# One piece of every expert's weights is loaded as nine row combs instead of one block

## The chip, the cores and the metric

The kernel runs on one core of a Trainium2 chip. The metric is the device time of one execution, in microseconds (us). Three runs of the kernel before gave 1218.85, 1219.08 and 1220.23 us, a median of 1219.08 us. "GB/s" is what the core's 16 DMA engines moved together.

## The reference, cut to what matters

A two-layer decoder trunk over 256 tokens of width 1024, all in float32. The first layer has latent attention and a dense SwiGLU, the second one sliding-window attention and a mixture of eight SwiGLU experts, of which each token uses two. The part that the change touches is the last one:

```python
D_MODEL, SEQ, N_EXPERTS, TOP_K, D_FF_EXPERT = 1024, 256, 8, 2, 3584

def moe(xn, w_router, w_gate, w_up, w_down):
    logits = (xn @ w_router).astype(jnp.float32)
    top_val, top_idx = lax.top_k(logits, TOP_K)
    top_w = jax.nn.softmax(top_val, axis=-1)
    gates = jnp.sum(jax.nn.one_hot(top_idx, N_EXPERTS, dtype=jnp.float32) * top_w[..., None], axis=-2)

    def per_seq(args):
        xs, gs = args
        hg = jnp.einsum('sd,edf->sef', xs, w_gate)
        hu = jnp.einsum('sd,edf->sef', xs, w_up)
        hh = jax.nn.silu(hg) * hu * gs[..., None].astype(xs.dtype)
        return jnp.einsum('sef,efd->sd', hh, w_down)

    return lax.map(per_seq, (xn, gates))
```

All eight experts get tokens, so all their weights are read: 8 experts x 3 matrices x 1024 x 3584 float32 numbers, 352 MB.

## The kernel before, in words

The first 400 us are attention, the dense layer and the router. The rest is the expert phase. There an item is one expert with up to 96 gathered tokens. Its weights come as 24 pieces (`pieces`, line 558) of 128 partitions x 3584 numbers, 1792 KB each: pieces 0 to 7 are the gate matrix, 8 to 15 the up matrix, 16 to 23 the down matrix (four for each half of the hidden width). A piece is one row of 14336 contiguous bytes for each partition. The pieces go round a ring in SBUF that holds eight of them (`LAPS`), so a piece can be loaded once the piece eight before it has been read by TensorE.

SyncE (SP) issues all of these loads, in order, in `load_item` (line 700). `room_for` makes it wait until TensorE has read the piece that lay there. The load itself is line 718; only the last piece, number 23, is split into two halves by columns (lines 721 and 722), the second of which counts on a semaphore of its own, `tail_landed`. Every load adds 16 to the semaphore of its ring place (`landing(m, first)`) when it has landed. Each of the DMA engines that carry a load adds one to it behind its own rows; I call such an addition a mark.

TensorE (PE) works item by item (`pe_item`, line 1638): products with gate (line 1575), with up (the same line), then the down product in 28 rows of 1024 columns, `down` at line 1603, 14 rows, the gather for the next item (line 1541), and 14 more rows. In a narrow item (at most 64 tokens) a down row is two matmuls, lines 1618 and 1619; in a wide one it goes through `wide_step` (lines 1550 to 1554). A down row waits for the pieces that it needs: row 14 is the first of piece 20, row 21 the first of piece 22, row 24 the first that reads piece 23, and rows 26 and 27 read its second half. VectorE and ScalarE make the hidden activations between the up and the down product (lines 2113 and 2118).

ScalarE issues loads of its own at the start (lines 823 to 835), on another queue of the same DMA engines: eight tables of 16, 16, 8, 3, 2, 1, 8 and 8 rows, one row for each partition, and the 256 positions, one number at a time. At the end it issues a quarter of the output, 128 rows.

The program has eight items in this execution; the first one (`load_item(0, 0, True)`) has four of its pieces in other places, loaded ahead, and the other seven are a loop.

Of the kernel before, what the change touches and what calls it, by code (L numbers as in the profile page):

```python
# [37 lines left out]
P = 128  # L38
# [91 lines left out]
class Semaphores:  # L130
    def __init__(self, sem):
# [125 lines left out]
        self.ahead_loaded_b = sem("ahead_loaded_b")  # L257
        self.ahead_loaded_c = sem("ahead_loaded_c")
        self.tail_landed = sem("tail_landed")
        self.gu_read = sem("gu_read")  # L260
        self.gate_mm = sem("gate_mm")
        self.sg_ready = sem("sg_ready")
# [21 lines left out]
def build(nc, x, positions, w_in, g_q, g_kv, w_uq, w_ukv, w_o, kv_g, kv_w, kv_b, swa_w_q, swa_b_q,  # L284
          swa_sinks, swa_w_o, swa_b_o, rel_bias, g_attn, g_ffn, f_gate, f_up, f_down, w_router,
          e_gate, e_up, e_down, g_final, consts, out):
    with ExitStack() as ctx:
# [12 lines left out]
        s = Semaphores(lambda name: ctx.enter_context(nc.semaphore(name)))  # L300
# [257 lines left out]
        pieces = [(kind, 0, k) for kind in "gu" for k in range(KD)]  # L558
        pieces += [("d", half, part) for half in range(2) for part in range(TILES * D // PIECE)]
        NP = len(pieces)  # L560
        DOWN0 = 2 * KD
        assert NP % LAPS == 0 and KD == LAPS
        ppos = {p_: m for m, p_ in enumerate(pieces)}
        whole = ring[:].rearrange("p a n -> p (a n)")

        def turn_of(m, first):

            return sum(1 for p_ in range(m) if p_ not in AHEAD) if first else m - OUTSIDE

        def place(m, first):  # L570

            return PIECE * ((FIRST_AT + turn_of(m, first)) % LAPS)

        def landing(m, first):

            return s.piece_landed[turn_of(m, first) % LAPS]
# [5 lines left out]
        def piece_here(eng, i, m, first):  # L582

            if first and m in AHEAD_A:
                eng.wait_ge(s.ahead_loaded_a, 16 * len(AHEAD_A))
            elif first and m in AHEAD_B:
                eng.wait_ge(s.ahead_loaded_b, 16)
            elif first and m in AHEAD_C:
                eng.wait_ge(s.ahead_loaded_c, 16)
            else:  # L590
                eng.wait_ge(landing(m, first), i * (16 * NP // LAPS) + 16 * (turn_of(m, first) // LAPS + 1))

        def piece(m, first):
            if first and m in AHEAD:
                return AHEAD[m]
            return whole[:, place(m, first):place(m, first) + PIECE]

        def down_row(r):

            c0 = (place(DOWN0, False) + D * r) % (LAPS * PIECE)  # L600
            return whole[:, c0:c0 + D]

        def down_pieces(r):

            return range(DOWN0 + D * r // PIECE, DOWN0 + (D * r + D - 1) // PIECE + 1)

        def last_down_row(m):

            return (PIECE * (m + 1 - DOWN0) - 1) // D

        def in_tail(r):

            return D * r + D > PIECE * (NP - DOWN0) - PIECE // 2

# [45 lines left out]
        def _(sp):  # L660
# [11 lines left out]
            def piece_of_expert(m, expert):  # L672
                kind, half, part = pieces[m]
                if kind == "d":
                    return ed[:, expert, half, part * PIECE:(part + 1) * PIECE]
                return (eg if kind == "g" else eu)[:, expert, part, :]

            def room_for(i, m, first):

                if first and turn_of(m, True) < LAPS:  # L680
                    for sl in dense_under(m):
                        if sl >= 5:
                            sp.wait_ge(*used_up(NU - 1))
                        else:
                            sp.wait_ge(*stream[earlier_fill(DENSE, sl)][4:6])
                    return
                if not first and m < LAPS:
                    sp.wait_ge(s.down_mm, i * (2 * TILES) + (last_down_row(m + 2 * LAPS) + 2 - 2 * TILES))
                    return
                under = m - LAPS  # L690
                if first:
                    in_ring = [p_ for p_ in range(NP) if p_ not in AHEAD]
                    under = in_ring[in_ring.index(m) - LAPS]
                kind, _, k = pieces[under]
                if k < KD - 1:
                    sp.wait_ge(s.gu_read, i * (2 * KD - 2) + ((KD - 1) * (kind == "u") + k + 1))
                else:
                    sp.wait_ge(s.gate_mm if kind == "g" else s.up_mm, i * (2 * THIRDS) + 2 * THIRDS)

            def load_item(i, expert, first):  # L700
                for m in range(NP):
                    if first and m == 5:
                        sp.wait_ge(s.spT_mm, AH)
                        for ma, room in AHEAD_A.items():
                            sp.dma_start(room, piece_of_expert(ma, expert)).then_inc(s.ahead_loaded_a, 16)
                        sp.wait_ge(s.spv_mm, MH)
                        for ma, room in AHEAD_B.items():
                            sp.dma_start(room, piece_of_expert(ma, expert)).then_inc(s.ahead_loaded_b, 16)
                    if first and m == LAPS + 1:
                        sp.wait_ge(s.swo_mm, 4)  # L710
                        sp.wait_ge(s.router_mm, 2)
                        for ma, room in AHEAD_C.items():
                            sp.dma_start(room, piece_of_expert(ma, expert)).then_inc(s.ahead_loaded_c, 16)
                    if first and m in AHEAD:
                        continue
                    room_for(i, m, first)
                    if m < NP - 1:
                        sp.dma_start(piece(m, first), piece_of_expert(m, expert)).then_inc(landing(m, first), 16)
                    else:
                        src, mid = piece_of_expert(m, expert), PIECE // 2  # L720
                        sp.dma_start(piece(m, first)[:, 0:mid], src[:, 0:mid]).then_inc(landing(m, first), 16)
                        sp.dma_start(piece(m, first)[:, mid:PIECE], src[:, mid:PIECE]).then_inc(s.tail_landed, 16)

            load_item(0, 0, True)
            sp.wait_ge(s.counts_ready, 1)
            sp.wait_ge(s.order_ready, 1)
            with sp.Fori(1, NE) as i:
                load_item(i, sp.value_load(order[0:1, bass.ds(i, 1)], min_val=0, max_val=NE - 1), False)
# [8 lines left out]
            rows = out[0].rearrange("(t p) d -> t p d", p=P)  # L737
# [348 lines left out]
        def _(pe):  # L1086
# [39 lines left out]
            for half in range(2):  # L1126
# [22 lines left out]
                for t in range(TT):  # L1149
                    for k in range(3):  # L1150
                        r = w[:, k, :].rearrange("p (h n) -> p h n", n=192)[:, :, NOPE:192]
# [21 lines left out]
            for n in range(4):  # L1173
                t, half = n // 2, n % 2
                for k in range(2):
                    r = w[:, k, :].rearrange("p (h n) -> p h n", n=256)[:, 4 * half:4 * half + 4, NOPE:256]
# [370 lines left out]
            def wide_step(bank, slots, left, right, first, last):  # L1547
                thirds = [slots[:, 32 * j:32 * j + 32] for j in range(3)]
                for j in range(3):
                    pe.matmul(ps[32 * j:32 * j + 32, bank, :], thirds[j], left, start=first, stop=last)  # L1550
                pe.matmul(ps[SLOTS:P, bank, :], thirds[2], right, start=first, stop=last)  # L1551
                for j, cols in ((0, 0), (1, 0), (0, LASTQ), (1, LASTQ)):
                    q = 32 * j + cols // 4
                    mm = pe.matmul(ps[q:q + 32, bank + 1, 0:LASTQ], thirds[j], right[:, cols:cols + LASTQ], start=first, stop=last)  # L1554
                return mm
# [47 lines left out]
            def down(i, half, j, narrow, first_item):  # L1603
                r = half * TILES + j
                for m in down_pieces(r):
                    if r == 0 or m not in down_pieces(r - 1):
                        piece_here(pe, i, m, first_item)
                if in_tail(r) and not in_tail(r - 1):
                    pe.wait_ge(s.tail_landed, i * 16 + 16)
                if r == 0:  # L1610
                    pe.wait_ge(s.sgt_ready, i + 2)
                if j == 0:
                    pe.wait_ge(s.hhT_ready, i * 2 + (half + 1))
                w = down_row(r)
                first, last = r == 0, r == 2 * TILES - 1
                if narrow:
                    lhs = hhT[:, half, j, 0:NARROW]
                    pe.matmul(ps[0:NARROW, DOWN_BANK, :], lhs, w[:, 0:512], start=first, stop=last)  # L1618
                    mm = pe.matmul(ps[64:64 + NARROW, DOWN_BANK + 1, :], lhs, w[:, 512:1024], start=first, stop=last)  # L1619
                else:  # L1620
                    mm = wide_step(DOWN_BANK, hhT[:, half, j, :], w[:, 0:512], w[:, 512:1024], first, last)
                mm.then_inc(s.down_mm, 1)
# [555 lines left out]
```

## Time and profile before

| What | us |
|---|---|
| median of three runs | 1219.08 |
| the profiled execution | 1220.05 |
| its span, first to last instruction | 1218.2 |
| TensorE busy in the span | 1167.6 |
| share of the DMA engines' time, SP's loads | 82.1% |
| expert phase, rate of the DMA engines | about 425 GB/s |

The span is 1.85 us shorter than the execution's own time. The row of tenths for DMA in the page has a 9 for each slice from the fifteenth to the last but one, and TensorE has 8 or 9 in the same slices, so the shares of busy time alone don't say which of the two sets the time. That is read from waits and from the times at which loads landed. An issue's time to landing runs from SP's issue to the last mark of the load, so with many loads queued it is mostly time in the queue.

### The profile page before, as it was taken

To read this page: it belongs to the slowest core of one execution; us is meant where nothing else is said; L and a number is where in the kernel's file an instruction comes from. 1 tells how busy PE (TensorE), PEld (TensorE's weight loads), DVE (VectorE), ACT (ScalarE), POOL (GpSimd) and SP (SyncE) were. 2 spreads that over 40 slices of the span, in tenths; PEclk is the share of its full clock that TensorE was granted. 3 is DMA by queue.
4 is the path that set the end of the run, shared out by engine and by line. 5 is a ranking of instruction groups with operands and counts; after the bars stand their busy time and mean duration, and the time that the engine had idled before them with its cause. 6 is when DMAs were issued, how large, how long until landed. Compare 5 with 4: busy or idle time off the path is not lost.

```text
span 1218.2 us, 21794 instructions
## 1 busy us (share of the span) xinstructions
PE 1167.6 (96%) x9461; PEld 586.6 (48%) x9462; DVE 338.9 (28%) x727; ACT 213.2 (17%) x399; POOL 36.0 (3%) x67
## 2 busy tenths in 40 slices
PE   7999999999999999899899999899999889999987
PEld 4878777778765534233233433333343233334323
DVE  3666566666272302101002011010201101020112
ACT  2454333333263100000010010101010010101001
POOL 2130000000200000000000000000000000000000
PEclk9999999999999999899899999999999999999999
DMA  9624645237535899999999999999999999999994
GB/s 339 244 69 162 230 161 188 89 139 257 219 122 241 358 425 406 420 428 425 425 425 426 417 421 426 426 426 426 424 426 425 426 427 426 424 425 408 427 426 171
DMA packets 56044, 413.42 MB, mean 339 GB/s; under 512 B 4703, under 2 KB 10077, under 8 KB 32141
## 3 DMA queue, kind: packets, MB, share of 16 engines
q1 hardware_dynamic: 54464, 410.40, 82.1%
q8 instruction: 81, 1.33, 0.4%
q0 software_dynamic: 944, 1.29, 0.3%
q10 hardware_dynamic: 540, 0.29, 0.1%
q14 instruction: 15, 0.11, 0.0%
HBM read 410.91 MB, written 1.05 MB: 338 GB/s over the span
## 4 chain that ended last, share of the span: by engine, by line
PE 82%; DMA 9%; DVE 4%; issue 2%; ACT 2%; ACTq 0%; POOL 0%; POOLq 0%; DVEq 0%; SPq 0%
PE ps L1575 35%; PE ps L1550 6%; PE ps L1618 6%; DMA ring<-in_moe_w_gate 5%; DMA ring<-in_moe_w_down 4%; PE ps L1262 4%; PE ps L1258 4%; PE ps L1259 4%; PE ps L1554 3%; PE ps L1593 3%; PE ps L1434 2%; PE ps L1541 2%; PE ps L1385 2%; PE ps L1121 2%; ACT w_hi L918 1%
## 5 line engine op out<-in xcount | busy, mean ns | idle before, releaser
L1575 PE MATMUL ps<-ring,arena 128*32 128x448 f32 x4736 | 460.9, 548 | 11.4 <-issue 7.1
L1575 PEld LDWEIGHTS ps<-ring,arena 128*32 128x32 f32 x4736 | 154.3, 111 | 310.5 <-issue 307.3
L1618 PE MATMUL ps<-ring,arena 128*64 128x512 f32 x280 | 125.3, 601 | 15.0 <-DMA ring<-in_moe_w_down 11.0
L1619 PE MATMUL ps<-ring,arena 128*64 128x512 f32 x280 | 125.3, 602 | 0.0
L2113 DVE TENSOR_TENSOR arena<-arena,ps 128x448 f32<-128x448 f32 x38 | 22.3, 603 | 285.1 <-PE ps L1575 284.7
L1550 PE MATMUL ps<-ring,arena 128*32 128x512 f32 x504 | 87.0, 593 | 2.4 <-DVE arena L2118 2.4
L1859 DVE TENSOR_TENSOR w_lo<-ring,w_hi 128x2048 fp32r<-128x2048 f32 x31 | 71.0, 2292 | 57.1 <-ACT w_hi L918 55.1
L1551 PE MATMUL ps<-ring,arena 128*32 128x512 f32 x168 | 85.9, 593 | 0.0
L1618 PEld LDWEIGHTS ps<-ring,arena 128*64 128x64 f32 x280 | 37.4, 138 | 96.1 <-issue 71.4
L918 ACT CAST w_hi<-ring 128x2048 fp32r<-128x2048 f32 x31 | 59.1, 1909 | 112.6 <-PE ps L1262 112.6
L2095 DVE TENSOR_TENSOR h<-h,ps 128x512 f32<-128x512 f32 x36 | 24.7, 687 | 175.5 <-PE ps L1593 175.5
L1258 PE MATMUL ps<-w_hi,xT_hi 128*128 128x512 f32 (+1 forms) x176 | 64.9, 376 | 0.0
L1259 PE MATMUL ps<-w_hi,xT_lo 128*128 128x512 f32 (+1 forms) x176 | 63.9, 370 | 0.0
L1030 ACT ACTIVATE arena<-ps 128x448 f32<-128x448 f32 x38 | 20.7, 544 | 246.1 <-PE ps L1575 245.4
L1037 ACT ACTIVATE arena<-ps,vecT 128x96 f32<-128x96 f32 x36 | 9.3, 342 | 309.0 <-PE ps L1541 309.0
L1554 PE MATMUL ps<-ring,arena 128*32 128x256 f32 x672 | 51.7, 379 | 0.0
L1554 PEld LDWEIGHTS ps<-ring,arena 128*32 128x32 f32 x672 | 21.8, 110 | 50.3 <-issue 50.3
L1262 PE MATMUL ps<-w_lo,xT_hi 128*128 128x512 f32 (+1 forms) x176 | 41.4, 379 | 0.0
L2129 DVE TENSOR_TENSOR arena<-ps,vecT 128x384 f32<-128x384 f32 x8 | 4.5, 557 | 119.5 <-PE ps L1541 119.5
L1619 PEld LDWEIGHTS ps<-ring,arena 128*64 128x64 f32 x280 | 37.4, 138 | 0.0
L1541 PEld LDWEIGHTS ps<-arena,xn 128*128 128x128 f32 x288 | 34.5, 200 | 5.6 <-issue 5.3
L1258 PE MATMUL ps<-w_hi,fhhT_hi 128*128 128x512 f32 x88 | 34.7, 395 | 1.4 <-DVE h L1928 1.4
(309 smaller groups left out, 1193.9 us busy)
## 6 DMA issues: line engine op xcount, KB each, us to landing
ring<-in_moe_w_gate SPq DMA_DIRECT2D x63, 1792.0 KB, 18.9
ring<-in_moe_w_up SPq DMA_DIRECT2D x61, 1792.0 KB, 18.4
ring<-in_moe_w_down SPq DMA_DIRECT2D x56, 1792.0 KB, 20.9
ring<-in_moe_w_down SPq DMA_DIRECT2D x16, 896.0 KB, 21.2
ring<-in_ffn_w_gate SPq DMA_DIRECT2D x5, 2048.0 KB, 7.9
ring<-in_ffn_w_up SPq DMA_DIRECT2D x5, 2048.0 KB, 7.7
ring<-in_ffn_w_down SPq DMA_DIRECT2D x5, 2048.0 KB, 7.9
ring<-in_mla_w_o SPq DMA_DIRECT2D x2, 2048.0 KB, 24.8
```

The source lines that it names most:

```text
L918: act.copy(hi, w).then_inc(s.whi_ready, 1)
L1258: pe.matmul(out, lhs[0][:, k, c], rhs_hi[:, k, :], start=(first and k == 0), stop=False)
L1259: pe.matmul(out, lhs[1][:, k, c], rhs_hi[:, k, :], start=False, stop=False)
L1262: mm = pe.matmul(out, lhs[0][:, k, c], rhs_lo[:, k, :], start=False, stop=(last and k == nk - 1))
L1541: mm = pe.matmul(ps[:, GATHER_BANK + k // 4, (k % 4) * SLOTS:(k % 4 + 1) * SLOTS], xn[:, t, k * P:(k + 1) * P], sel[:, t, :], start=(t == ...
L1550: pe.matmul(ps[32 * j:32 * j + 32, bank, :], thirds[j], left, start=first, stop=last)
L1551: pe.matmul(ps[SLOTS:P, bank, :], thirds[2], right, start=first, stop=last)
L1554: mm = pe.matmul(ps[q:q + 32, bank + 1, 0:LASTQ], thirds[j], right[:, cols:cols + LASTQ], start=first, stop=last)
L1575: mm = pe.matmul(ps[Q * q:Q * q + Q, bank_of(a, j), 0:CH], lhs, w[:, c0:c0 + CH], start=first, stop=last)
L1618: pe.matmul(ps[0:NARROW, DOWN_BANK, :], lhs, w[:, 0:512], start=first, stop=last)
L1619: mm = pe.matmul(ps[64:64 + NARROW, DOWN_BANK + 1, :], lhs, w[:, 512:1024], start=first, stop=last)
L1859: dve.tensor_tensor(lo, w, hi.bitcast(F32), ALU.subtract).then_inc(s.wlo_ready, 1)
```

## The change

Piece 22, the last but one, is no longer one load of 128 rows. Seven loads take the partitions 0, 8, ..., 120, then 1, 9, ..., 121, and so on to 6, 14, ..., 126: 16 rows each, 8 partitions apart. Two more take the 16 rows that are left, in two sets of 8 rows 16 partitions apart: 7, 23, ..., 119 and 15, 31, ..., 127. The first of the nine counts on the piece's own semaphore, the other eight on a new one, `comb_landed`. TensorE waits for both before the first down row that reads the piece. The same bytes go from the same place to the same place, and nothing is computed otherwise.

```diff
         NP = len(pieces)
+        COMBED, TEETH = NP - 2, 8
+        FULL_COMBS = [slice(r, P, TEETH) for r in range(TEETH - 1)]
+        HALF_COMBS = [slice(r, P, 2 * TEETH) for r in (TEETH - 1, 2 * TEETH - 1)]
+        COMBS = FULL_COMBS + HALF_COMBS
         DOWN0 = 2 * KD
...
                     room_for(i, m, first)
-                    if m < NP - 1:
+                    if m == COMBED:
+                        room, src = piece(m, first), piece_of_expert(m, expert)
+                        for rows in COMBS:
+                            sp.dma_start(room[rows, :], src[rows, :]).then_inc(landing(m, first) if rows == COMBS[0] else s.comb_landed, 16)
+                    elif m < NP - 1:
                         sp.dma_start(piece(m, first), piece_of_expert(m, expert)).then_inc(landing(m, first), 16)
...
                     if r == 0 or m not in down_pieces(r - 1):
                         piece_here(pe, i, m, first_item)
+                        if m == COMBED:
+                            rest = 16 * (len(COMBS) - 1)
+                            pe.wait_ge(s.comb_landed, i * rest + rest)
```

On SP, in the body of the loop over the experts, pieces 21, 22 and 23 stood as follows before (lines 718, 721 and 722 are the loads, ISA rows set up registers or wait):

```order
L718 DMA ring<-in_moe_w_down 128x3584
L696 REGISTER_ALU
L718 ISA
L718 DMA ring<-in_moe_w_down 128x3584
L721 ISA
L721 DMA ring<-in_moe_w_down 128x1792
L722 ISA
L722 DMA ring<-in_moe_w_down 128x1792
```

In the changed kernel the same place reads so (line 725 is the comb's load, 730 and 731 the halves of piece 23):

```order
L727 DMA ring<-in_moe_w_down 128x3584
L701 REGISTER_ALU
L725 ISA
L725 DMA ring<-in_moe_w_down 16x3584
...
L725 DMA ring<-in_moe_w_down 8x3584
L725 ISA
L725 DMA ring<-in_moe_w_down 8x3584
L730 ISA
L730 DMA ring<-in_moe_w_down 128x1792
L731 ISA
L731 DMA ring<-in_moe_w_down 128x1792
```

Eight more loads and their register instructions now stand ahead of piece 23.

On PE, in the narrow branch of the loop, the first down row that reads piece 22 stood so before, with what it waits for (`piece_landed2` is the semaphore of the piece's ring place):

```order
L1619 MATMUL ps<-ring,arena 64x512
L1618 MATMUL ps<-ring,arena 64x512 [waits piece_landed2]
L1619 MATMUL ps<-ring,arena 64x512
L1618 MATMUL ps<-ring,arena 64x512
```

And now:

```order
L1631 MATMUL ps<-ring,arena 64x512
L1619 ISA [waits piece_landed2]
L1630 MATMUL ps<-ring,arena 64x512 [waits comb_landed]
L1631 MATMUL ps<-ring,arena 64x512
L1630 MATMUL ps<-ring,arena 64x512
```

One instruction that only waits has come ahead of the matmul; nothing else moved on PE, and nothing on the other engines.

## Rows read from the trace of the kernel before

**Rows 1.** The page: the DMA engines in 40 slices.
```profile
DMA  9624645237535899999999999999999999999994
GB/s 339 244 69 162 230 161 188 89 139 257 219 122 241 358 425 406 420 428 425 425 425 426 417 421 426 426 426 426 424 426 425 426 427 426 424 425 408 427 426 171
```
**Rows 2.** Busy time by stretch: length, each engine, PE's clock, DMA share, GB/s.
```profile
core 0: us, PE busy (x) PEld busy (x) DVE busy (x) ACT busy (x) POOL busy (x), PEclk, DMA share, GB/s
789.02:893.63 104.61, 103.59 (x1070) 39.45 (x1074) 12.66 (x21) 5.17 (x13) 0.00 (x0) 0.98 1.01 425
893.63:998.24 104.61, 96.93 (x858) 35.18 (x850) 11.45 (x20) 7.78 (x15) 0.00 (x0) 1.00 1.01 426
485.00:1182.00 697.00, 669.53 (x6350) 244.70 (x6346) 82.39 (x140) 43.49 (x89) 0.00 (x0) 0.99 1.01 424
```
**Rows 3.** SP's loads on line 718: issue to landing, whole span, then 485 to 1172 us.
```profile
DMA to landing us min/median/max: 7.1/19.3/32.1
DMA to landing us min/median/max: 9.2/20.5/32.1
```
**Rows 4.** The chain of waits: start us, us, what (a load: issue to landing).
```profile
761.43 27.59 DMA ring<-in_moe_w_gate
943.42 23.14 DMA ring<-in_moe_w_down
967.98 30.26 DMA ring<-in_moe_w_gate
1155.49 26.73 DMA ring<-in_moe_w_down
```
**Rows 5.** DMA queues from 789.02 to 998.24 us: packets, MB, share of 16 engines.
```profile
q1 hardware_dynamic: 7249, 88.76, 100.2%
q8 instruction: 16, 0.26, 0.5%
```
**Rows 6.** The single loads issued at 940.27 and 1152.49: KB, us to landing.
```profile
ring<-in_moe_w_down SPq DMA_DIRECT2D x1, 1792.0 KB, 22.0
ring<-in_moe_w_down SPq DMA_DIRECT2D x1, 1792.0 KB, 23.6
```
**Rows 7.** Last item's piece 23: SP's timeline, then each half's KB and us to landing.
```profile
1171.01 0.33 SPq L721 DMA_DIRECT2D ring<-in_moe_w_down  x1
1171.53 0.33 SPq L722 DMA_DIRECT2D ring<-in_moe_w_down  x1
ring<-in_moe_w_down SPq DMA_DIRECT2D x1, 896.0 KB, 30.2
ring<-in_moe_w_down SPq DMA_DIRECT2D x1, 896.0 KB, 31.9
```
**Rows 8.** The page: ScalarE's queue: packets, MB, share of 16 engines.
```profile
q10 hardware_dynamic: 540, 0.29, 0.1%
```
**Rows 9.** TensorE's timeline at the last item's down rows.
```profile
1182.27 0.76 PE L1618 MATMUL ps<-ring,arena 128*64 128x512 f32 x1 [2.45 <-DMA ring<-in_moe_w_down]
...
1182.82 1.06 PE L1618 MATMUL ps<-ring,arena 128*64 128x512 f32 x1
...
1183.67 1.06 PE L1618 MATMUL ps<-ring,arena 128*64 128x512 f32 x1
...
1204.21 0.59 PE L1618 MATMUL ps<-ring,arena 128*64 128x512 f32 x1
...
1204.64 0.59 PE L1618 MATMUL ps<-ring,arena 128*64 128x512 f32 x1
```
**Rows 10.** Busy time by stretch, as Rows 2, in the last item.
```profile
1182.00:1186.00 4.00, 3.73 (x10) 1.16 (x12) 0.00 (x0) 0.00 (x0) 0.00 (x0) 0.58 1.03 437
1186.00:1190.00 4.00, 4.00 (x20) 1.15 (x16) 0.00 (x0) 0.00 (x0) 0.00 (x0) 0.99 0.98 416
```
**Rows 11.** TensorE's waits for loads: total us, times, longest us.
```profile
PE ps L1618 <- DMA ring<-in_moe_w_down: 11.0, 7, 2.4
PE ps L1575 <- DMA ring<-in_moe_w_gate: 4.4, 2, 2.2
```

More of the change, by code:

```diff
@@ L259, in __init__ @@
         self.tail_landed = sem("tail_landed")
+        self.comb_landed = sem("comb_landed")
         self.gu_read = sem("gu_read")
```

## The prediction, written before the changed kernel ran

> **What bounds the kernel now.** First the page, its slices by time: from the fifteenth slice to the last but one the DMA engines are busy nine tenths or more and move 402 to 430 GB/s [rows 1]. Then busy time by stretch: from 485 to 1182 us the DMA share is 1.01 at 424 GB/s, while TensorE is busy 669.5 of 697 us, so it has 27.5 us to spare and the DMA engines have none [rows 2]. Then the times to landing: in that stretch no load landed sooner than 9.2 us after its issue, and the fastest of all, which had no queue ahead of it, took 7.1 [rows 3]. So work was always queued. The end of the last load is set by how fast the queue drains, and TensorE's waits for loads are only 15.4 us in all [rows 11], because the ring lets it run behind or catch up. What ends last is the stream of weights.
>
> Then how evenly it drains. The chain of waits gives the landings of two experts' first gate pieces: 761.43 + 27.59 = 789.02 and 967.98 + 30.26 = 998.24, two experts apart [rows 4]. That is 104.61 us for one expert. Two neighbouring plain pieces landed at 940.27 + 22.0 = 962.3 and 943.42 + 23.14 = 966.56, 4.3 us apart [rows 4, 6], so 24 of them need 103.2 us. The slowest engine loses the other 1.4 us of each expert. It shows as single steps: 1152.49 + 23.6 = 1176.1 and 1155.49 + 26.73 = 1182.22 are 6.1 us apart, 1.8 more than plain [rows 4, 6]. Beside the weights there are 16 instruction packets in two experts, 0.26 MB [rows 5], so eight for an expert of 16 KB each. Spread evenly they would cost each of 16 engines 8 KB, which at 426/16 = 26.6 GB/s is 0.3 us. A loss of 1.4 us on the slowest says that some engines carry them all. A piece has landed when its slowest engine is done, so the others run ahead by about 1.1 us (1.4 less 0.3) for each expert or more, and their lead is worth nothing.
>
> **The change part by part.**
> *Rows on engines.* A plain piece is 128 rows on 16 engines, eight each, 4.3/8 = 0.54 us a row. How many engines a small load uses can be counted. ScalarE's queue has 540 packets [rows 8]: 62 table rows, 256 positions and 128 output rows are 446, and 94 are left, which is 16+16+8+3+2+1+8+8 for the tables and 16+16 for the other two. So a load of 16 rows leaves 16 marks, one of 8 rows leaves 8. A full comb gives each engine one row. The two half combs give one half of the engines two rows and the other half none: nine rows against seven, where all had eight. The Trainium skill has this rule too ("DMA: Bandwidth & Descriptors", "Why a DMA increments its semaphore by 16 and not by 1"), and adds that SyncE's loads take the lowest-numbered engines; by that, the seven-row half would always be the same one. The packets agree with the count; which engines they are no row shows.
> If the half that gets seven rows is the one that carries the instructions, the slowest engines gain 0.54 us for each expert; if it is the other, they lose it.
> *More loads.* Seven marks instead of one on an engine with seven rows, nine on the others. Piece 23 is already two loads: its halves landed at 1171.01 + 30.2 = 1201.2 and 1171.53 + 31.9 = 1203.4, 2.2 apart against 4.3/2 = 2.15 [rows 7]. So an extra load costs an engine between 0 and 0.1 us, and I take 0.02, since the halves differ from half a piece by less than the reading's last digit. Six extra: 0.12, leaving 0.54 - 0.12 = 0.42 us gained for each expert (between 0 and 0.54).
> *Rate of a combed row.* The trace has no large load of fewer than 128 partitions, so it bounds nothing here but by its plain rows: 0.54 us at best, and if engines stand in each other's way two by two, 1.07. I take 0.54, the row's measured price, for the forecast; the other end is a rival below.
> *Issue.* SP's two halves are issued 1171.53 - 1171.01 = 0.52 apart [rows 7]; eight more loads are 4.2 us of SP. Behind them stand piece 23 and, for the next expert, piece 0. Piece 23 was issued about 3 us after piece 22, held by TensorE's reading, so it comes 9 x 0.52 - 3.0 = 1.7 us later. What hides it is the queue: loads took a median of 20.5 us to land where 7.1 would do [rows 3]; at the tightest, 9.2, 2.1 us of cover are left. Without it, up to 1.7 us per expert.
> *The wait on PE.* `comb_landed` holds down rows 21 to 27 and all products behind them. It comes due when the last comb row lands, as the old wait did, and the waiting instruction is one of some 1650: nothing beyond the landing itself.
>
> *The end.* In the last item TensorE starts its down row at 1182.27 after waiting 2.45 us for piece 18 [rows 9], and from there computes without a wait for loads to 1206. Seven combs lie ahead of that piece: 7 x 0.42 = 2.9 us. After that wait TensorE's granted clock reads 0.58 for 4 us, next to 0.99 behind it [rows 10]: between 1.2 and 2.4 GHz, mostly the lower, with the engine idle before it. A step there takes 1183.67 - 1182.82 = 0.85 us instead of 1204.64 - 1204.21 = 0.43 [rows 9], 1.7 us in those 4 us. A wait shortened by the earlier arrival (it was one of several; the engine then gets there earlier too) may not cost the clock: 0 to 1.4 us, as then the last half of piece 23, landing 8 x 0.42 = 3.4 us earlier at 1200.0, becomes what row 26 waits for (it starts at 1204.21 now [rows 9]). I take 0.8.
> Sum: 2.9 + 0.8 = 3.7 us less. Against the profiled execution's 1220.05 that is 1216.4. The median of the runs is 0.97 below that execution, so I forecast 1215.5 us in its terms, own range 1213 to 1218.
>
> **Rivals.**
> *The combs collide (slower).* In a plain piece each engine's rows lie in partitions that no other engine writes. A comb hands its rows to engines in another pattern, and the 16 rows may lie in fewer places of SBUF than there are engines. Its place is piece 22; it decides as soon as two engines that share a place are slowed by more than the 0.42 us gained. If all comb rows take double, an engine with nine rows needs 18 row times instead of 8: 5.4 us more, 103.2 + 5.4 = 108.6 against 104.6, 4.0 for each expert, 32 over eight: 1251. Half of that where some pairs are out of step (1235), and more where engines knocked out of order then meet in the plain pieces (1262). For it: nothing in the trace contradicts it, and the rate of 26.6 GB/s for an engine may as well be that of the place it writes. Against it: no row shows it. The Trainium skill says exactly this ("SBUF — State Buffer", "Door 1: The DMA port swizzle"): 16 ports, each of 8 partitions in two groups of four 32 apart, at 27.2 GB/s each. By its table partitions 8 apart reach 8 of the 16 ports, which makes the doubling above; no run here shows it.
> *The wrong half.* The nine-row half is the one with the instructions: 0.54 + 8 x 0.02 = 0.70 more for each expert, seven of them ahead of piece 18: 4.9 us, 1224. For it: the rows leave the half open. Against it: only the skill's numbering, which doesn't say where instructions travel either.
> *Nothing to see.* An extra load costs nearer 0.09 than 0.02, six of them eat the 0.54, or SP's 4.2 us empty the queue where it is short: 1219. For it: the reading allows up to 0.1 for a load. Against it: the halves' 2.2.
>
> **How the numbers follow.** Forecast 0.45, collision 0.32, wrong half 0.09, nothing 0.14. What a measurement can tell from no change is about 0.2%, 2.4 us. Of the forecast's 0.45, 0.04 lie within it (a gain of under 2.4): faster 0.41, same 0.14 + 0.04 = 0.18, slower 0.41. The range must reach from the forecast's lower end to deep in the collision: 1213 to 1262 leaves out the worst of the knock-on and a gain of over 6. The cases have both signs: the likeliest's own range is 1213 to 1218.
>
> **What would show it.** Right: first gate pieces of neighbouring experts land 104.2 us apart instead of 104.61, GB/s by stretch rises from 425 to 426 or 427, TensorE's wait before 1182 is under 2.45. Collision: in each expert one stretch of some 10 us with the GB/s well under 400 where piece 22 is moved, and experts 107 to 110 us apart. Wrong half: 105.3 us apart with no dip. The issue term is wrong if the DMA share falls under 1 behind piece 22. The whole is wrong if TensorE, and not a landing, ends the wait ahead of most down rows.

## The result, and the profile after

| | before | after |
|---|---|---|
| median of the runs | 1218.96 us (4 runs, 1218.83 to 1220.23) | 1311.43 us (4 runs, 1300.29 to 1312.42) |
| ratio | | 1.0731, interval 1.0709 to 1.0753: slower |
| span of the profiled execution | 1218.2 us | 1310.6 us |

The forecast was 1215.5 us with a range of 1213 to 1262. The kernel lost 92 us and lies outside the range, on the side of the rival "the combs collide", but 49 us past its worst figure. Three of the four runs lie between 1310.9 and 1312.4 us and one at 1300.3; nothing here explains that one, and a single run of a changed kernel can therefore be off by some 12 us.

The page's DMA slices (as [rows 1], a slice is now 32.8 us), then TensorE's longest waits for loads (us in total, times, longest; lines 1584 and 1630 are 1575 and 1618 of the kernel before):

```profile
DMA  9516444348159999999999999999999999999991
GB/s 342 203 62 249 160 169 161 129 161 313 58 231 374 415 330 425 428 319 426 426 379 346 425 428 274 419 425 371 317 426 426 290 388 401 406 284 426 425 313 67
```
```profile
PE ps L1630 <- DMA ring<-in_moe_w_down: 53.4, 22, 5.9
PE ps L1584 <- DMA ring<-in_moe_w_up: 25.4, 25, 1.2
PE ps L1584 <- DMA ring<-in_moe_w_gate: 10.6, 10, 2.4
```

The busy row of the DMA engines has not changed: nines to the end. The GB/s row has: where before it stood at 425, there is a dip every three or four slices, eight in all, one for each expert. Whoever reads only the busy share sees nothing. TensorE waits 89.4 us for loads where it waited 15.4 [rows 11]. The chain of waits gives the landings of first gate pieces of every other expert, as in [rows 4]:

```profile
558.20 37.88 DMA ring<-in_moe_w_gate
...
787.72 43.52 DMA ring<-in_moe_w_gate
...
1025.66 43.00 DMA ring<-in_moe_w_gate
```

They land at 596.08, 831.24 and 1068.66 us: 117.6 and 118.7 us an expert where it was 104.61. Inside a dip (SyncE's comb loads of this expert start at 674.97), busy time by stretch:

```profile
core 0: us, PE busy (x) PEld busy (x) DVE busy (x) ACT busy (x) POOL busy (x), PEclk, DMA share, GB/s
660.00:676.00 16.00, 16.00 (x176) 5.52 (x172) 0.41 (x1) 0.00 (x0) 0.00 (x0) 1.00 1.00 425
...
684.00:688.00 4.00, 4.00 (x56) 1.65 (x52) 0.09 (x1) 0.00 (x0) 0.00 (x0) 1.00 0.97 201
...
696.00:700.00 4.00, 4.00 (x47) 2.52 (x40) 0.00 (x0) 0.00 (x0) 0.00 (x0) 1.00 1.00 253
...
704.00:708.00 4.00, 4.00 (x52) 1.56 (x48) 0.00 (x0) 0.00 (x0) 0.00 (x0) 1.00 0.99 419
```

201 GB/s is half of 425, the engines are busy all the while (0.97), and the stretch lasts some 22 us (680 to 702, 242 GB/s on average). Piece 22 has 1.8 MB, which at half rate is 8.7 us. So two things are to be explained: the half rate, and why it lasts more than twice as long as the piece.

### The profile page after: what moved, and what is told of

Its sections match the earlier page's. It is cut to its first block, busy times and chain, and to the rows that moved or that the text cites. A ratio compares the mean times of both kernels' runs of the same rounds, so it can differ in the third digit from the quotient of the medians.

```text
span 1310.6 us, 21978 instructions
## 1 busy us (share of the span) xinstructions
PE 1186.2 (91%) x9461; PEld 584.6 (45%) x9462; DVE 339.0 (26%) x727; ACT 213.1 (16%) x399; POOL 36.0 (3%) x67
## 4 chain that ended last, share of the span: by engine, by line
PE 63%; DMA 29%; DVE 3%; issue 2%; ACT 2%; ACTq 0%; POOL 0%; POOLq 0%; DVEq 0%; SPq 0%
PE ps L1584 25%; DMA ring<-in_moe_w_gate 12%; DMA ring<-in_moe_w_down 10%; DMA ring<-in_moe_w_up 7%; PE ps L1559 4%; PE ps L1271 4%; PE ps L1267 4%; PE ps L1268 4%; PE ps L1630 3%; PE ps L1443 2%; PE ps L1563 2%; PE ps L1602 2%; PE ps L1394 2%; PE ps L1130 2%; PE ps L1550 1%
## 5 line engine op out<-in xcount | busy, mean ns | idle before, releaser
L1584 PEld LDWEIGHTS ps<-ring,arena 128*32 128x32 f32 x4736 | 151.0, 111 | 349.3 <-issue 286.8
L1630 PE MATMUL ps<-ring,arena 128*64 128x512 f32 x280 | 141.0, 656 | 54.5 <-DMA ring<-in_moe_w_down 53.4
L1631 PE MATMUL ps<-ring,arena 128*64 128x512 f32 x280 | 141.0, 656 | 0.0
L1630 PEld LDWEIGHTS ps<-ring,arena 128*64 128x64 f32 x280 | 39.6, 150 | 149.3 <-issue 75.6
L1563 PEld LDWEIGHTS ps<-ring,arena 128*32 128x32 f32 x672 | 21.8, 110 | 50.3 <-issue 50.3
L1631 PEld LDWEIGHTS ps<-ring,arena 128*64 128x64 f32 x280 | 39.6, 150 | 0.0
```

Source lines behind the costliest of these rows:

```text
L1584: mm = pe.matmul(ps[Q * q:Q * q + Q, bank_of(a, j), 0:CH], lhs, w[:, c0:c0 + CH], start=first, stop=last)
```

## The experiments

The theories. A: the 16 rows of a comb lie in fewer places of SBUF (sets of partitions that are filled through one door) than there are engines, and each place takes in only what one engine brings. B: the same on the side of the weights in HBM. C: the number of loads (or SyncE's issues, or marks). D: the split of 9 rows to 7. Later K and U: engines that are out of step (some of them behind the others in the queue) make a comb dearer than by itself. In the run with one comb, K stands for another thing, that every comb costs the same.

**Patterns by themselves.** A kernel of loads only, four pieces for each pattern; the kernel's computation is left out. The pattern is a list of row slices:

```python
COMB8 = every(8, 16, range(8))              # eight loads of 16 partitions, 8 apart
BLOCK = every(1, 16, range(0, P, 16))       # eight loads of 16 adjacent partitions
LOW_COMB = every(16, 8, range(16))          # sixteen loads of 8 partitions, 16 apart
LOW_SPREAD = every(4, 8, [b + r for b in (0, 32, 64, 96) for r in range(4)])   # 8 partitions, 4 apart
# columns: seven loads of 128 partitions x 512 columns
```

> This kernel leaves out all of the reference's computation: SyncE alone issues loads of the down weights, four pieces (1792 KB each) for each of eleven patterns, one pattern after the other with a wait between them, and stores x as its output. Theory A (engines that write into the same one of 16 groups of partitions share that group's rate): plain pieces 4.3 us each; eight combs of 16 rows 8 apart 8.4 each (8 groups reached); the same combs read from blocks of 16 adjacent rows also 8.4; blocks of 16 adjacent partitions 16.9 (4 groups); combs 7 apart about 6.8, read from rows 8 apart the same; 8-row loads 4 apart 8.6, 8-row loads 16 apart 16.9; columns 4.6 to 4.9; 64 rows 8.4; 112 and 16 rows 6.8. Theory B (the rows read in memory collide, not those written): the pattern of the source decides, so combs read from blocks differ from combs read from combs, and combs 7 apart read from rows 8 apart are as slow as combs 8 apart. Theory C (each further load costs an engine time): the time goes by the number of loads alone: 8 loads a piece all alike, whatever the spacing, columns with 7 as slow as they, 64 rows with 2 nearly plain.

SyncE's timeline (start us, length of the issues; the next pattern starts when all has landed), and the page's slices of 10.9 us:

```profile
5.62 1.87 SPq L32 DMA_DIRECT2D ring<-in_moe_w_down  x4
25.15 20.18 SPq L33 DMA_DIRECT2D ring<-in_moe_w_down  x32
61.80 20.09 SPq L34 DMA_DIRECT2D ring<-in_moe_w_down  x32
98.09 14.98 SPq L35 DMA_DIRECT2D ring<-in_moe_w_down  x32
158.25 19.85 SPq L36 DMA_DIRECT2D ring<-in_moe_w_down  x32
192.09 19.82 SPq L37 DMA_DIRECT2D ring<-in_moe_w_down  x32
225.38 43.11 SPq L38 DMA_DIRECT2D ring<-in_moe_w_down  x64
271.92 38.77 SPq L39 DMA_DIRECT2D ring<-in_moe_w_down  x64
339.73 14.00 SPq L40 DMA_DIRECT2D ring<-in_moe_w_down  x28
362.26 4.97 SPq L41 DMA_DIRECT2D ring<-in_moe_w_down  x8
399.21 3.88 SPq L42 DMA_DIRECT2D ring<-in_moe_w_down  x8
431.73 0.41 SPq L66 DMA_DIRECT2D out<-res  x1
```
```profile
GB/s 245 429 230 213 221 168 210 213 187 128 127 126 126 128 145 241 228 178 247 231 149 162 170 165 146 114 109 113 114 109 113 242 391 192 216 217 171 261 231 196
```

From one start to the next, divided by four: plain 4.9 us a piece, combs 9.2 (33), combs fed from adjacent rows of the weights 9.1 (34), adjacent blocks 15.0 (35), combs 7 apart 8.5 (36; 8.3 from other source rows, 37), eight-row combs 4 apart 11.6 (38, held by SyncE, which issues 64 loads in 43.1 us), eight-row combs 16 apart 17.0 (39), strips of columns 5.6 (40), two loads of 64 rows 9.2 (41), 112 and 16 rows 8.1 (42). The rates are levels: 429, then about 213, then 127, then 109 to 114. B falls (33 and 34 agree) and so does C (28 strips are nearly as fast as plain). What counts is which partitions a load covers. If combs lie in eight places and eight-row combs 16 apart in four, a place takes in 27 GB/s (213/8, 110/4), which is what one engine carries (425/16). Here "The Trainium skill" ("SBUF — State Buffer", "Door 1: The DMA port swizzle") states 16 ports of 27.2 GB/s; combs and eight-row combs agree, adjacent blocks (127 GB/s, by that page four ports) lie 17% above it. Which partitions share a place no run here maps out.

The trace also has the time of each row's packet (14 KB), and it shows the collision without the issues of SyncE and without the wait at a pattern's end. The median is 0.54 us in plain pieces, 1.09 in combs (1.08 when fed from adjacent rows), 1.80 in adjacent blocks, 1.10 in two loads of 64 rows. Eight-row combs 4 apart take 0.54 and eight-row combs 16 apart 1.09, with the same number of loads, rows and marks. So an engine is not slow in small loads as such, and not in every partition that it does not write in a plain piece, or blocks would cost a row no more than combs do. A's sizes hold less well: combs 7 apart were expected at 6.8 us a piece and took 8.5, the 112 and 16 rows at 6.8 and took 8.1, blocks at 16.9 and took 15.0.

**The kernel with other patterns.** Against after, only the lists of row slices change, and in one run the source rows:

```diff
# e1_eight_full_combs
-        HALF_COMBS = [slice(r, P, 2 * TEETH) for r in (TEETH - 1, 2 * TEETH - 1)]
+        FULL_COMBS = [slice(r, P, TEETH) for r in range(TEETH)]; HALF_COMBS = []
# e2_seven_apart
+        FULL_COMBS = [slice(r, 7 * 16, 7) for r in range(7)]
+        HALF_COMBS = [slice(7 * 16 + r, P, 2) for r in range(2)]
# e3_combs_from_blocks: comb n is loaded from 16 (or 8) adjacent rows of the weights
-    sp.dma_start(room[rows, :], src[rows, :])
+    sp.dma_start(room[rows, :], src[block_rows, :])
# e4_three_loads: as e2, the seven combs as one load
+        FULL_COMBS = [slice(0, 7 * 16)]
# e6_blocks
+        FULL_COMBS = [slice(16 * r, 16 * r + 16) for r in range(8)]; HALF_COMBS = []
```

> Eight combs of 16 rows, 8 partitions apart, and no 8-row loads: each engine has eight rows of piece 22 again. Theory A (shared groups of partitions): still slow, 1290 to 1320 us, since the combs are what collides. Theory D (the nine-and-seven split put more work on the slow half, or loads of 8 rows are slow themselves): back to 1219 to 1225. Theory C (number of loads): about 1300, like the changed kernel with its nine.

1312.0 us, one run like all of this group (before on that chip 1221.3). Nothing gained by leaving out the half combs: D falls.

> The changed kernel with its seven 16-row combs 7 partitions apart (they cover partitions 0 to 111) and the two 8-row loads on partitions 112 to 127; number and size of the loads are the same. Theory A: it moves, because the rows of a comb now lie in 14 groups instead of 8, but engines no longer meet the same partner from row to row, so somewhere between 1265 and 1305 us. Theory C (number of loads or marks): unchanged, 1308 to 1315. Theory D (nine and seven): unchanged, 1308 to 1315.

1320.1 us, outside what A expected, and 5 us outside what C and D did. In the quiet kernel (loads only) combs 7 apart had missed A's figure too, but were no dearer than combs 8 apart (8.5 against 9.2). So the miss is one of size, and the kernel adds something to a pattern's own cost.

> The changed kernel with the same destination rows in each load, but read from as many adjacent rows of the weights (the down product is then computed with rows of piece 22 in another order). Theory A (write side): unchanged, 1300 to 1315 us. Theory B (read side: rows 448 KB apart in memory collide): back to 1215 to 1225.

1314.9 us: B falls in the kernel too. (The rows of piece 22 then lie in another order, so this kernel computes something else than the reference; its loads and their times are what is compared.)

> Piece 22 as one load of partitions 0 to 111 (seven adjacent rows for an engine) and two loads of 8: three loads instead of nine, and each engine writes the same rows in the same order as in the run with combs seven apart (1320 us). Theory A: about 1320 again. Theory C (number of loads): a third of the cost, about 1250 or less.

1315.6 us with three loads instead of nine, as A expected; C's figure was 1250.

> Piece 22 as eight loads of 16 adjacent partitions: an engine still writes one row of each, but the 16 rows of a load lie in 4 places instead of 8. By itself such a piece took 15.0 us against 4.9 plain and 9.2 combed. Theory A: at least 8 x 10.2 = 81 us over the kernel before, 1300 or more, up to 1330. A rule that only strides are slow (a load of adjacent partitions is fast): 1222, as the strips.

1304.1 us. Blocks by themselves are 2.4 times as dear as combs (10.2 us over plain against 4.3) and in the kernel no dearer (one run, within the 1300 to 1312 us of the combed kernel's own). The half of A that says "slow" holds, the half that gives sizes does not.

**As many loads, other cut.**

```diff
-    for rows in COMBS: sp.dma_start(room[rows, :], src[rows, :])
+    for n in range(8): sp.dma_start(room[:, 448 * n:448 * n + 448], src[:, 448 * n:448 * n + 448])
```

> Piece 22 of each expert as eight loads of 128 partitions x 448 columns: as many loads and marks as eight full combs, but rows on engines as in a plain piece. Theory A (pattern of partitions): within 0.5% of the kernel before, 1216 to 1226 us (eight loads more would be at most 7 x 0.1 x 8 = 5.6 us). Theory C (the number of loads in a piece, or what SyncE spends on issuing them, makes the cost): near the 1312 us of the combs.

1221.78 us against 1219.55, ratio 1.0019 (1.001 to 1.0029). Eight loads cost almost nothing when the partitions are as in a plain piece. C falls for good, and the price of a load is had: in the strips' chain of waits

```profile
775.30 14.45 DMA ring<-in_moe_w_gate
...
985.58 14.20 DMA ring<-in_moe_w_gate
...
1160.65 27.15 DMA ring<-in_moe_w_down
```

two experts take 999.78 - 789.75 = 210.03 us, 0.4 an expert more than 104.61, for seven extra loads: 0.06 each.

**One comb piece alone.** Strips in all experts, eight full combs in the fourth only, then in the seventh only.

```diff
-    with sp.Fori(1, NE) as i: load_item(i, ...)
+    with sp.Fori(1, 3) as i: load_item(i, ...)          # 6 in the second kernel
+    load_item(3, ..., combed=True)
+    with sp.Fori(4, NE) as i: load_item(i, ...)
```

> As the strips, but the fourth expert's piece 22 alone is eight full combs. Theory A with nothing behind it: 4.2 us over the strips. Theory K, each comb costs the same by itself: (1312 - 1219) / 8 = 11.6 us over the strips. Theory G (the cost grows from comb to comb, as engines drift further apart): under 11.6 here, and the landings after it return to 4.3 us a piece.

1232.54 us, ratio to before 1.0106 (1.0089 to 1.0123), 10.8 over the strips. By landings, in its chain:

```profile
762.10 35.89 DMA ring<-in_moe_w_gate
...
993.88 14.20 DMA ring<-in_moe_w_gate
```

797.99 is 8.2 behind the strips' 789.75, and two experts later 1008.08 is 8.3 behind 999.78. One comb costs 8.2 us and stops costing. That is twice the piece by itself, and less than the 11.5 of after. The profiled run was the fastest of the four, 8.6 over the strips' profiled run; by the median alone K's 11.6 would not be excluded, and what excludes it is the landings of the next run and e1's chain.

> As the run with one comb piece in the fourth expert, but it is in the seventh. By itself there it cost 8 to 9 us by the landings behind it, with the engines 5 us apart before it; in the run with eight combed experts the costs grew from 7 (first) to 16 us (seventh), while the distance between first and last engine grew from 3 to 20 us. Theory U (what counts is how far engines are apart, which combs themselves enlarge): about 8 to 10 here, as engines are 7 us apart, 1230 to 1233. Theory L (late experts are dearer for another reason): 16, 1238.

1232.05 us (1.0106, 1.009 to 1.0123); piece 19 of its last expert lands at

```profile
1165.24 31.50 DMA ring<-in_moe_w_down
```

1196.74, 8.9 behind the strips' 1187.80. (The whole span is 10.7 behind. The other 1.8 come at the end: TensorE's granted clock reads 0.83 and 0.74 from 1195 to 1203 us, after a wait, and in the strips' run 1.00.) Late experts are not dearer by themselves. Combs behind combs are, as e1's chain shows:

```profile
556.69 37.24 DMA ring<-in_moe_w_gate
...
784.10 40.52 DMA ring<-in_moe_w_gate
...
1018.15 43.84 DMA ring<-in_moe_w_gate
```

824.62 and 1061.99 are 35.6 and 63.8 us behind [rows 4]: the first four combs cost 8.9 each, the next two 14.1 each. Meanwhile the sixteen engines' landing events for a first gate piece spread over 5, 7, 10, 14, 20 us from expert to expert, where the strips' spread over 3 to 8. From expert to expert these pieces land 113.0, 114.4, 116.3, 117.7, 119.7 and 121.0 us apart (strips 105.1). The change's own nine loads rise faster and level off: 113.7, 115.9, 119.3, 118.5, 118.9, 116.8.

**Out of step, in quiet.** Loads only again, 24 pieces a phase, each phase waited for as a whole.

```python
run([P_] * 24)                              # L72
run([P_] * 11 + [C_] + [P_] * 12)           # L73, C_: eight full combs
run([P_] * 11 + [C_] * 2 + [P_] * 11)       # L74
run([P_] * 11 + [H_] + [P_] * 12)           # L75, H_: the change's nine loads
run([SKEW] + [P_] * 24)                     # L76, SKEW: eight loads of 8 rows; then L77 to L79
```

> SyncE alone, nothing else runs; eight phases of 24 pieces, eleven pieces in flight, each phase waited for as a whole: (1) 24 plain; (2) a piece of eight full combs in the middle; (3) two such pieces in a row; (4) the change's own nine loads in the middle; (5) eight loads of 8 rows first, then 24 plain; (6) the same with a full-comb piece in the middle; (7) the same with the change's nine loads; (8) sixteen loads of 8 rows first and a full-comb piece. Theory A (places in SBUF are shared by engines while a comb is written, nothing else): 24 plain about 24 x 4.3 + 3 = 106 us; a comb +4.2, two +8.4, the nine loads +6.3; phase 5 +4.3 over phase 1 and phases 6, 7 +8.5 and +10.6. Theory K (knock-on: after a comb, or once engines are out of step, plain pieces behind it are slow too): a comb costs well over 4.2, up to the 11.5 us that an expert lost in the kernel, and two in a row cost less than twice one; engines out of step before it (6 to 8) make it dearer than (2).

```profile
5.75 60.01 SPq L72 DMA_DIRECT2D ring<-in_moe_w_down  x24
111.31 68.13 SPq L73 DMA_DIRECT2D ring<-in_moe_w_down  x31
221.36 74.53 SPq L74 DMA_DIRECT2D ring<-in_moe_w_down  x38
336.86 71.44 SPq L75 DMA_DIRECT2D ring<-in_moe_w_down  x32
448.33 72.31 SPq L76 DMA_DIRECT2D ring<-in_moe_w_down  x32
561.81 77.85 SPq L77 DMA_DIRECT2D ring<-in_moe_w_down  x39
680.10 78.14 SPq L78 DMA_DIRECT2D ring<-in_moe_w_down  x40
```

Starts give 105.6 us plain, 110.0 with a comb piece (+4.5), 115.5 with two (+9.9), 111.5 with the nine loads (+5.9). Engines in step pay just the comb: in the phase with two, the slices of 2.89 us show it, six of them at half rate, 17 us for two pieces of 8.7, and nothing behind.

```profile
GB/s 213 412 407 435 422 422 452 412 452 412 427 442 412 437 422 427 447 204 214 219 219 214 209 372 422 432 427 422 437 417 432 432 417 432 427 427 432 427 427 144
```

Phase L77 stood 4.8 above L76, and L78 (the nine loads) 6.1: no knock-on, it seemed.

The next run made four engines, or one, late in the same way:

> SyncE alone again, 24 pieces a phase; ahead of each phase some engines are made late by small loads: (1) eight loads of 4 rows, so that four engines are eight rows (4.3 us) late, then 24 plain; (2) the same, seventh piece in full combs; (3) the same, seventh and eighth in full combs; (4) four loads of 4 rows, then 24 plain; (5) the same with one comb piece; (6) eight loads of 1 row, so one engine is late, 24 plain; (7) with one comb piece; (8) as (1) with the change's own nine loads. Theory U (a comb's price depends on which engines are out of step with which, with no rule but that two engines on one place share its rate of one engine; worked out with that rule alone): comb +8.2 in (2), two combs +8.3 in (3), +6.2 in (5), +4.1 in (7), +8.8 in (8). Theory A alone (a comb costs what it costs in step): +4.5, +9.9, +4.5, +4.5, +5.9, as measured with the engines in step.

Differences of 3.8 (one comb), 7.9 (two), 3.3, 6.3 and 6.3: on neither theory. The fault is in the experiment. The small loads stood at a phase's start, where the queue is empty, and SyncE issues one in 0.6 us while an engine carries a row in 0.54. How late the engines were can be read from the time between the first and the last landing mark of a plain piece: 2.3 us in b2's L76, and in this run 1.3 with the comb but 2.8 without it (phases L75 and L74), so the two phases differ in more than the comb. Only the last pair but one (one engine, 3.3 us late in both phases) compares like with like, and there a comb cost 6.3. The other pairs tell little of engines out of step. Put behind three plain pieces, the small loads queue up:

```diff
-    run([E4] + [P_] * 24)
+    run([P_] * 3 + [E4] + [P_] * 21)                       # likewise SKEW, E1
+    run([P_] * 3 + [E4] + [P_] * 6 + [C_] + [P_] * 14)
```

> SyncE alone, 24 pieces a phase; now the small loads stand behind three plain pieces, so that the queue is never empty and the engines that carry them do get late: (1) eight loads of 8 rows (eight engines 4.3 us late) and plain pieces; (2) with one full-comb piece; (3) eight loads of 4 rows (four engines 4.3 us late), plain; (4) with one comb piece; (5) with two; (6) with the change's nine loads; (7) eight loads of 1 row, plain; (8) with one comb piece. Theory U (price of a comb depends on which engines are out of step; worked out with the one rule that two engines on one place share the rate of one): (2) - (1) = 4.1, (4) - (3) = 8.2, (5) - (3) = 8.3, (6) - (3) = 9.2, (8) - (7) = 4.1. Theory A alone, as in step: 4.5, 4.5, 9.9, 5.9, 4.5.

```profile
5.84 64.11 SPq L74 DMA_DIRECT2D ring<-in_moe_w_down  x32
115.57 76.66 SPq L75 DMA_DIRECT2D ring<-in_moe_w_down  x39
234.63 70.08 SPq L76 DMA_DIRECT2D ring<-in_moe_w_down  x32
346.66 78.79 SPq L77 DMA_DIRECT2D ring<-in_moe_w_down  x39
466.62 83.90 SPq L78 DMA_DIRECT2D ring<-in_moe_w_down  x46
590.79 82.07 SPq L79 DMA_DIRECT2D ring<-in_moe_w_down  x40
713.88 70.54 SPq L80 DMA_DIRECT2D ring<-in_moe_w_down  x32
825.22 77.56 SPq L81 DMA_DIRECT2D ring<-in_moe_w_down  x39
942.88 0.40 SPq L82 DMA_DIRECT2D out<-res  x1
```

By the marks of the plain pieces ahead of the comb, the engines are now 4.6 us apart with eight made late, 4.4 with four and 6.3 with one (meant were 4.3 each time), where L73 of b2 had 0.5. With eight engines late a comb piece costs 119.06 - 109.73 = 9.3 us, with four late 7.9 (two pieces 12.1, the change's nine loads 11.1), with one late 6.3; in step it was 4.5. That engines out of step raise the price is shown, with nothing else running, though each phase ran once. Behind the comb piece the marks stand 5.4, 4.4 and 8.0 us apart, and 6.2 behind the nine loads: most of these pieces leave the engines further apart than they found them. Theory U's one rule gives one of the sizes (8.2 for 7.9) and misses the others (4.1 for 9.3, 8.3 for 12.1, 9.2 for 11.1, 4.1 for 6.3), low each time.

**In step, in the kernel.** SyncE waits for piece 21 before it issues piece 22.

```diff
     if m == COMBED:
+        piece_here(sp, i, m - 1, first)
```

> The strips (1221.8 us), but SyncE waits for piece 21 to land before it issues piece 22, so that all engines are idle and then start piece 22 together. An unqueued load took 7.1 us against 4.3 of moving, so 2.8 us idle each time: 1221.8 + 8 x 2.8 = 1244 us. This is the base for the next run.

> Eight full combs (1312 us without the wait), with the same wait before them. Theory U: the engines start the combs in step, so a comb piece costs 4.5 us as by itself: 1244 + 8 x 4.5 = 1280, and the added wait makes the kernel faster. Theory V (the 11.5 us of an expert come from something else of the kernel, such as TensorE's and VectorE's traffic in SBUF, whatever the engines' step): 1244 + 92 = 1336.

Strips 1254.54 us (1.0287, 1.027 to 1.0304), 11 more than expected: the wait costs 4.1 us an expert, not 2.8. Around one such wait the DMA share is 0.46 and 0.64 in two stretches of 4 us: the first loads behind it are issued no faster than they are carried (eight strips in 3.95 us). Combs 1271.11 us (1.0426, 1.0408 to 1.0443). Adding a wait made the combed kernel 41 us faster (1312 to 1271). In their chains, strips first, then combs:

```profile
793.46 19.61 DMA ring<-in_moe_w_gate
...
1011.22 19.84 DMA ring<-in_moe_w_gate
```
```profile
800.79 20.61 DMA ring<-in_moe_w_gate
...
1023.20 20.58 DMA ring<-in_moe_w_gate
```

109.0 and 111.2 us an expert. The combs cost 2.2 us, and the marks of a first gate piece now stand 0.3 to 1.9 us apart. That 2.2 is below their own 4.5, and U's 1280 us too high by 9, would follow if strips behind a wait do not run at full rate either, as the DMA share says; it was not tried by itself. V, which put 11.5 us on something else of the kernel, is out by 65 us.

No kernel here beats the one before, and nothing measured points to one that would.

## Why the prediction was wrong

- **What bounds the kernel: right.** The stream of weights bounded it before and does after; a loss in it came out at the end whole. TensorE's timeline has the wait for the last expert's piece 18, which ended at 1182.27 [rows 9], now here:

```profile
1269.22 1.12 PE L1630 MATMUL ps<-ring,arena 128*64 128x512 f32 x1 [5.58 <-DMA ring<-in_moe_w_down]
```

87.0 us later with seven comb pieces ahead of it, 12.4 each; the eighth, with what it delays, makes the 92.4 at the end.
- **"Rate of a combed row", the step that failed.** It was taken at 0.54 us, "the row's measured price", with 1.07 as the other bound. In step the stream falls to 204 to 219 GB/s, half of 425 to 430, and a combed row's packet takes 1.09 us: the upper bound. What spoke for 0.54 was that rows had been measured at it and that no row showed a collision, though every row measured was one of a plain piece, which could show none. The nearest row that could speak was the rate itself: 26.6 GB/s for an engine may be its own or its place's, which the text said and then put in a rival.
- **The rival's size: too small.** "4.0 for each expert" was 5.9 for the change's nine loads in step and 11.5 in the kernel. Even in step it was short, because it set 1.4 us of lead against the loss. The knock-on was named (1262) and taken to be at most 1.4 us an expert more. Measured, it is about half of the 11.5 (5.6 us; 7.1 with eight full combs, 4.5 in step), and it grows over the first combs, while the engines get further apart.
- **"More loads": 0.02 us each, measured 0.06** (strips), within the stated 0 to 0.1. By this alone the change's gain of 0.54 - 6 x 0.06 = 0.18 us an expert would have been 1.5 us, no difference that can be measured.
- **Rows on engines, 9 to 7.** Whether the half that gets seven is the one with the instructions stays open; 1311.4 and 1312.0 (all engines eight) do not part.
- **Issue.** Right that the queue hides it: in the dip the DMA share stays at 0.97 to 1.10 and the engines are never short. The nine issues took longer than nine times 0.52:

```profile
674.97 7.10 SPq L725 DMA_DIRECT2D ring<-in_moe_w_down  x9
682.26 0.34 SPq L730 DMA_DIRECT2D ring<-in_moe_w_down  x1
```

7.29 us from the first to piece 23, 0.8 each.
- **The end and TensorE's clock.** The wait there grew instead of shrinking (5.58 us for 2.45), and behind it and behind the next one the granted clock reads 0.55 (1270 to 1274) and 0.57 (1277 to 1281), as it did before (0.58 in [rows 10]). The 0.8 us that the end was to gain did not come.
- **What would show it** was right for the collision in kind: one stretch of low GB/s where piece 22 moves. Its "some 10 us" were 22, and its "107 to 110 us apart" 117.6 and 118.7.
- **Readings.** The "402 to 430 GB/s" of [rows 1] are 406 to 428 there, and the sum gives 1215.4, not 1215.5; nothing rests on either.

What stays open: how large the knock-on is for a given pattern of lateness. It is shown that engines 3.3 to 6.3 us apart take a comb piece from 4.5 to between 6.3 and 9.3 us, that a single one in the kernel, where the marks ahead of it stand 4.5 to 8 us apart, costs 8.2 to 8.9, and that removing the lateness takes most of it away. That the growth to 14 us in a row of combs comes from the spread of 10 to 20 us between engines fits, but was not tried by itself; nor was what makes blocks, dearest alone, no dearer than combs in the kernel.

## What to carry to other kernels

Give every load of weights all 128 partitions, and cut it by columns where it has to be cut: a piece of every expert in eight strips cost 2 us in all, in eight combs some 91. When a rate is said to be an engine's, ask what else would give the same number, and put the other answer's price into the forecast too. Read the GB/s row beside the busy row: in the dip the DMA share was 0.97 at 201 GB/s, so a DMA engine that moves half as much still counts as busy.

## What the runs showed of the hardware

- A comb of 16 partitions 8 apart runs at 213 GB/s, of 8 partitions 16 apart at 109 to 114, 16 adjacent partitions at 127, all 128 at 425 to 430. A 14-KB row takes its engine 1.09, 1.09, 1.80 and 0.54 us in them, and 0.54 in loads of 8 partitions 4 apart.
- Also loads of 64 adjacent partitions are slow: 9.2 us for a piece in two of them (L41 above), against 4.9.
- The same piece costs 4.5 us in combs with the engines in step, 6.3 to 9.3 with the engines 3.3 to 6.3 us apart, 14.1 behind four or five other combed experts.
- A wait that empties the queue costs 4.1 us and can pay: with it the combed kernel took 1271 us instead of 1312.
